# Dilated stage's maxima stored branch by branch, gate steps behind a block, two evictions ahead of a gate, blocks without a GpSimd drain

## The chip, the cores and the metric

The kernel runs on one core of one Trainium2 chip. The metric is the device time of one execution in microseconds, shown as the median of several runs.

## What is computed

One inference step of a one-layer hybrid decoder, for a prompt of 2048 tokens and 8 samples of 8 tokens, model width 1024, in float32. After an RMSNorm one projection `h @ w_in` gives the inputs of three mixers: an mLSTM matrix memory (4 heads of 64), a dilated window attention (6 heads of 64) and a stick-breaking attention (6 heads of 64). Their outputs go through `w_out`, an RMSNorm and the residual, then a squared-ReLU MLP of width 4096. The parts that the change touches, cut from the reference:

```python
# mLSTM: gates and chunk scan, chunks of 128 tokens
ig = ia + b_igate;  lf = log_sigmoid(fa + b_fgate)
b = cumsum(lf);     logw = where(causal, b[:, None] - b[None, :] + ig[None, :], -inf)
m_t = maximum(b + m, max(logw));  s = (q @ k.T) * exp(logw - m_t)
...
ya = rmsnorm(h_a) * g_mlstm * sigmoid(o_gate)

# dilated attention: three branches share q, k, v; joined by their softmax denominators
for window, dil in ((128, 1), (512, 4), (2048, 16)):
    s = (qs @ kk.T) * scale          # blocks of 128 queries x 256 keys, banded
    mx = max(s);  p = exp(s - mx);  den = sum(p)
    o = (p @ vv) / den;  lse = mx + log(den)
out = sum(softmax(lse over branches) * o)
```

## The kernel before

The program is a row of eight stages, each a `nc.Block` with its own semaphores. Within a block each engine has its own instruction list, written out by hand, and waits on semaphores. The stages in order: projection with the prompt's mLSTM (lines 111 to 990, names `p_`), stick-breaking of the prompt (`pc_`), dilated attention of the prompt (`pb_`), then three sample stages (`ms_`, `sd_`, `sc_`), the mixing with `w_out`, and the MLP. A block ends when every engine has drained and passed a barrier; then GpSimd clears the stage's semaphores (line 84) and a second barrier follows (line 85).

**Projection.** Three passes over 17 token tiles (16 of the prompt, one of the samples). A pass has the columns of one group of mixers, cut into three blocks `b` of 344 or 384 columns; a block is 24 matmuls, 8 slices of the width by three products of high and low parts, into one PSUM bank. ScalarE evicts each block (line 628) into `PT`, TensorE turns the q and k heads by three transposes a block (line 869), VectorE copies them out (line 787), and SyncE stores. In the first two passes blocks use four banks, in the third two, because the mLSTM chunks use the others.

The gate values of all chunks are prepared in the second pass, in steps that go to and fro between VectorE and TensorE. VectorE does a step at the end of its list of tiles 4, 6, 8, 10, 11, 12, 13 and 15, after the head copies of that tile; TensorE does the small matmuls `gates(0)` to `gates(4)` (lines 876 to 890) at the start of tiles 7, 9, 11, 12 and 13, each behind a wait on the count `pre_v` of VectorE. In the third pass tile `t` also carries chunk `t` of the mLSTM: ScalarE does `gate(t + 1)` (the output gate of the next chunk, three activations, which waits for that chunk's load) before the tile's evictions and `decay(t + 1)` (four activations, which waits for VectorE's `masked`) before the second. At tile 0 it does `gate(0)`, `decay(0)` and `gate(1)` first. Chunk 1's and chunk 2's loads go out when the second pass is done, since they land where its weights lie.

**Dilated attention.** Six heads. A head has three branches of 16 units, taken as 8 pairs each. For each head TensorE computes scores once for the maxima (`natural`, line 1705, branch by branch) and VectorE reduces them to `MX` (line 1647); this runs 36 pairs ahead of the second scores. The maxima of branch 0 and 1 must be put in the token order of branch 2, which is done through HBM: SyncE stores them into `scratch_bm` (one store for branch 0 with one number a packet, four for branch 1), waits for all five, and reads them back as `MR` (line 1480). VectorE joins them (`joint`, lines 1654 and 1658), SyncE stores the result and spreads it to `MB`, and the second scores subtract it. VectorE's list has `joint(0)` after pair 31, before the last four of the first 36. The queue of SyncE at the start of the stage:

```python
load_qk(1)
load_v(sp, 0, (2, 0))      # V of branch 2, V of branch 0; ScalarE issues branch 1's
for h in range(HB):
    if h >= 2:
        load_v(sp, h, (2, 0, 1))
    maxima(h)
    spread(h)
    ...
```

Of the kernel before, what the change touches and what calls it, by code (L numbers as in the profile page):

```python
# [14 lines left out]
P = 128  # L15
# [89 lines left out]
def project_phase(nc, A, S, O, F):  # L105
# [5 lines left out]
    with ExitStack() as ctx:  # L111
# [132 lines left out]
        qk_ok = m.sem("qk_ok")  # L244
        block = ctx.enter_context(nc.Block())

# [284 lines left out]
        def _(act):  # L531
# [57 lines left out]
            for v in range(3 * TILES):  # L589
# [12 lines left out]
                if p == 2 and t == 0:  # L602
                    act.wait_ge(mm_ok, 6 * TILES)
                    gate(0)
                    decay(0)
                if p == 2 and t + 1 < NCH:
                    gate(t + 1)
                for b, (a, e) in enumerate(PASSES[p]):
                    if b == 1 and p == 2:
                        if t >= 1:  # L610
                            norm(t - 1)
                        if t + 1 < NCH:
                            decay(t + 1)
                    if b == 2 and p == 0 and t + 1 < TILES:
                        high(t + 1)
                    if b == 0 and p == 0:
                        act.wait_ge(rs_ok, t + 1)
                    if b == 0 and v >= 2 and t < NT:
                        act.wait_ge(p_out[v % 2], stored(*divmod(v - 2, TILES)))
                    act.wait_ge(mm_ok, 3 * v + b + 1)  # L620
                    if t == NT:
                        if b == 2:
                            act.wait_ge(blk_ok, 3 * v + 1)
                        act.activation(lower(v, b, e - a), PP[bank(3 * v + b)][NS:P, 0:e - a], ACT.Copy, scale=rs[NS:P, t:t + 1]).then_inc(low_ok, 1)
                        continue
                    if b == 0 and t == 0 and p:
                        act.wait_ge(blk_ok, 3 * v)
                    act.activation(PT[v % 2][:, a - o:e - o], PP[bank(3 * v + b)][:, 0:e - a], ACT.Copy, scale=rs[:, t:t + 1]).then_inc(blk_ok, 1)  # L628
            state(act, 1)

# [217 lines left out]
        def _(pe):  # L848
# [100 lines left out]
            for v in range(3 * TILES):  # L949
                p, t = divmod(v, TILES)  # L950
                s = v % 3
                if p == 1 and t in (7, 9, 11, 12, 13):
                    gates((7, 9, 11, 12, 13).index(t))
                if p == 0:
# [4 lines left out]
                for b, (a, e) in enumerate(PASSES[p]):  # L959
# [4 lines left out]
                    for k in range(KD):  # L964
# [5 lines left out]
                        if t < NT:  # L970
                            ins = pe.matmul(out, HL[s][:, k, :], wh, start=False, stop=(k == KD - 1))  # L971
                    ins.then_inc(mm_ok, 1)
                    if b == 1 and p == 0 and t + 1 < TILES:
                        turn_tile(t + 1)
# [58 lines left out]
def stick_prompt_phase(nc, A, S, O, F, H):  # L1033
# [40 lines left out]
    with ExitStack() as ctx:  # L1074
# [38 lines left out]
        y_out = H.y_out  # L1113
        block = ctx.enter_context(nc.Block())

# [201 lines left out]
def dilated_prompt_phase(nc, A, S, O, T, H):  # L1317
# [61 lines left out]
    with ExitStack() as ctx:  # L1379
# [48 lines left out]
        y_out = T.y_out  # L1428
        block = ctx.enter_context(nc.Block())

# [29 lines left out]
        def _(sp):  # L1460
            def load_qk(h):
# [3 lines left out]
                for dst, src in ((Q[i], S["qkT"][GB + g]), (K[i], S["qkT"][GB + 3 + g])):  # L1465
                    for a in range(2):
                        sp.dma_start(dst[a * HD:(a + 1) * HD, :], src[d, 0:SEQ]).then_inc(qk_in[i], 16)

            def maxima(h):
                s = h % 2  # L1470
                sp.wait_ge(mx_ok, 2 * upto(h, 15))
                with nc.allow_non_contiguous_dma(reason="one maximum each"):
                    sp.dma_start(S["bm"][h, 0, :].rearrange("(n i) -> i n", i=P), MX[s][:, 0, :]).then_inc(m_out[s], 16)
                for n in range(4):
                    sp.dma_start(S["bm"][h, 1, n * 512:(n + 1) * 512].rearrange("(i f) -> i f", f=4),
                                 MX[s][:, 1, 4 * n:4 * n + 4]).then_inc(m_out[s], 16)
                sp.wait_ge(m_out[s], 16 * 5 * (h // 2 + 1))
                if h >= 2:
                    sp.wait_ge(mj_ok, h - 1)
                sp.dma_start(MR[s][:, :, :], S["bm"][h, 0:2, :].rearrange("b (p f) -> p b f", f=TILE)).then_inc(r_in[s], 16)  # L1480
# [21 lines left out]
            load_qk(1)  # L1502
            load_v(sp, 0, (2, 0))
            for h in range(HB):
                if h >= 2:
                    load_v(sp, h, (2, 0, 1))
                maxima(h)
                spread(h)
                if h == 0:
                    load_qk(2)  # L1510
                    load_v(sp, 1, (2, 0, 1))
                if h >= 2:
                    store(h - 2)
                if h >= 1 and h + 2 < HB:
                    load_qk(h + 2)
                if h == 4:
                    sp.wait_ge(T.padded, 1)
                    T.load(sp, A, S)
# [394 lines left out]
def mlstm_sample_phase(nc, A, S, O, W, T):  # L1913
# [6 lines left out]
    with ExitStack() as ctx:  # L1920
# [41 lines left out]
        y2_ok, y3_ok, yt_ps, yt_ok = (m.sem(x) for x in ("y2_ok", "y3_ok", "yt_ps", "yt_ok"))  # L1962
        block = ctx.enter_context(nc.Block())

# [265 lines left out]
def dilated_sample_phase(nc, A, S, O, W, G):  # L2230
# [12 lines left out]
    with ExitStack() as ctx:  # L2243
# [25 lines left out]
        passed = m.sem("passed")  # L2269
        block = ctx.enter_context(nc.Block())  # L2270

# [212 lines left out]
def stick_sample_phase(nc, A, S, O, W, G, E):  # L2484
# [9 lines left out]
    with ExitStack() as ctx:  # L2494
# [62 lines left out]
        y_out = E.s_out  # L2557
        block = ctx.enter_context(nc.Block())
        qs, ks = S["qkT"][GC:GC + 3, :, SEQ:SEQ + NS], S["qkT"][GC + 3:GC + 6, :, SEQ:SEQ + NS]
# [425 lines left out]
def mix_out_phase(nc, A, S, O, E):  # L2985


    with ExitStack() as ctx:
# [41 lines left out]
        x1_out, h_out = E.x1_out, E.h_out  # L3030
        block = ctx.enter_context(nc.Block())
        TILES = NT + 1
# [182 lines left out]
def mlp_phase(nc, A, S, O, E):  # L3215
# [72 lines left out]
    with ExitStack() as ctx:  # L3288
# [52 lines left out]
        y_out = m.sem("y_out")  # L3341
        block_ = ctx.enter_context(nc.Block())

# [590 lines left out]
```

## Time and profile before

| | us |
|---|---|
| median of 3 runs | 3605.03 |
| lowest, highest | 3599.06, 3608.02 |
| the profiled execution | 3601.67 |
| its span, first to last instruction | 3600.1 |

The profile is one execution. Its lines give engines as PE (TensorE), PEld (its weight loads), DVE (VectorE), ACT (ScalarE), POOL (GpSimd) and SP (SyncE); a `q` behind the name is the engine's sequencer, which also issues transfers. `L968` is line 968 of the kernel, `out<-in` are tiles, and a group in square brackets or behind a bar tells how long the engine stood idle before and what ended it. PEclk is the granted clock of TensorE, 1.00 at 2.4 GHz and 0.50 at 1.2 GHz.

### The profile page before, as it was taken

The numbers are of one execution on the slowest core, as the hardware profiler recorded it, in microseconds if no ns is written. First come the engines' busy times: TensorE is split into PE (matmuls) and PEld (weight loads), VectorE is DVE, ScalarE is ACT, GpSimd is POOL, SyncE is SP. The second block draws the span as 40 slices with busy tenths as digits, with TensorE's granted clock in tenths as the row PEclk, the third lists the DMA queues.
The fourth block names the chain that finished last, engine by engine and source line by source line (L and its number), as shares of the span: only waits on it lengthen the run. The fifth ranks groups of instructions, "written<-read, shape, count | busy, mean of one in ns | idle before, by whom it ended". The sixth has DMA issues, their size and how long they took to land. (4 is left out here: it accounts for less than half of the span.)

```text
span 3600.1 us, 61533 instructions
## 1 busy us (share of the span) xinstructions
PE 3375.1 (94%) x22189; PEld 2941.3 (82%) x22189; DVE 1951.7 (54%) x4014; ACT 1550.4 (43%) x3079; POOL 715.7 (20%) x994
## 2 busy tenths in 40 slices
PE   8999999989997999879989979999989999899997
PEld 7999999954444887456658769999989999899997
DVE  2211134469996442446665555666656565846564
ACT  3321122268884444235442235444454344545342
POOL 0111112146773345024430110000100000100000
PEclk9999999989997999999999989999999999999998
DMA  5664356521014542769975544343444343422222
GB/s 201 215 216 154 134 188 203 174 76 45 7 36 86 90 83 94 287 219 357 355 259 163 176 151 134 113 159 117 148 154 132 125 151 120 160 76 83 70 68 82
DMA packets 433980, 527.76 MB, mean 147 GB/s; under 512 B 93425, under 2 KB 370546, under 8 KB 429202
## 3 DMA queue, kind: packets, MB, share of 16 engines
q1 hardware_dynamic: 405236, 410.19, 37.1%
q10 hardware_dynamic: 12076, 63.43, 5.1%
q0 software_dynamic: 16384, 50.35, 3.8%
q8 instruction: 179, 2.93, 0.3%
q14 instruction: 105, 0.86, 0.1%
HBM read 430.08 MB, written 143.91 MB: 159 GB/s over the span
## 5 line engine op out<-in xcount | busy, mean ns | idle before, releaser
L3792 PE MATMUL p_DP<-p_UH,p_WH 128*128 128x352 f32 x1536 | 498.7, 325 | 20.4 <-issue 14.2
L3793 PE MATMUL p_DP<-p_UL,p_WH 128*128 128x352 f32 x1536 | 497.4, 324 | 0.0
L3794 PE MATMUL p_DP<-p_UH,p_WL 128*128 128x352 f32 x1536 | 497.2, 324 | 0.0
L3792 PE MATMUL p_UP<-fc_TH,p_WH 128*128 128x352 f32 x1344 | 438.5, 326 | 27.0 <-DVE p_WL L3690 15.1
L3793 PE MATMUL p_UP<-fc_TL,p_WH 128*128 128x352 f32 x1344 | 436.5, 325 | 0.0
L3794 PE MATMUL p_UP<-fc_TH,p_WL 128*128 128x352 f32 x1344 | 436.0, 324 | 0.0
L968 PE MATMUL p_PP<-p_WH,p_HH 128*128 128x384 f32 (+1 forms) x1224 | 419.4, 343 | 8.7 <-DVE p_HL L654 4.4
L969 PE MATMUL p_PP<-p_WL,p_HH 128*128 128x384 f32 (+1 forms) x1224 | 408.0, 333 | 0.0
L971 PE MATMUL p_PP<-p_WH,p_HL 128*128 128x384 f32 (+1 forms) x1152 | 384.0, 333 | 0.0
L3792 PEld LDWEIGHTS p_DP<-p_UH,p_WH 128*128 128x128 f32 x1536 | 291.5, 190 | 22.5 <-issue 20.6
L628 ACT ACTIVATE p_PT<-p_PP,p_rs 128x384 f32<-128x384 f32 (+1 forms) x144 | 82.2, 570 | 503.9 <-PE p_PP L971 503.9
L3731 DVE TENSOR_TENSOR p_acc<-p_DP,p_acc 128x352 f32<-128x352 f32 x336 | 171.0, 521 | 227.3 <-PE p_DP L3794 227.2
L3793 PEld LDWEIGHTS p_DP<-p_UL,p_WH 128*128 128x128 f32 x1536 | 291.7, 190 | 0.0
L3794 PEld LDWEIGHTS p_DP<-p_UH,p_WL 128*128 128x128 f32 x1536 | 291.3, 190 | 0.0
L3792 PEld LDWEIGHTS p_UP<-fc_TH,p_WH 128*128 128x128 f32 x1344 | 254.9, 190 | 31.4 <-DVE p_WL L3690 17.8
L1143 POOL TENSOR_TENSOR pc_W<-pc_G,pc_PR 128x512 f32<-128x512 f32 (+2 forms) x240 | 245.6, 1039 | 102.4 <-DVE pc_PR L1242 93.4
L3793 PEld LDWEIGHTS p_UP<-fc_TL,p_WH 128*128 128x128 f32 x1344 | 254.9, 190 | 0.0
L3794 PEld LDWEIGHTS p_UP<-fc_TH,p_WL 128*128 128x128 f32 x1344 | 254.8, 190 | 0.0
L968 PEld LDWEIGHTS p_PP<-p_WH,p_HH 128*128 128x128 f32 x1224 | 232.8, 190 | 12.7 <-DVE p_WL L644 5.8
L969 PEld LDWEIGHTS p_PP<-p_WL,p_HH 128*128 128x128 f32 x1224 | 233.1, 190 | 0.0
L787 DVE COPY p_QK<-p_QP 128x384 f32<-128x384 f32 (+1 forms) x85 | 49.6, 583 | 327.1 <-PE p_QP L869 327.1
L971 PEld LDWEIGHTS p_PP<-p_WH,p_HL 128*128 128x128 f32 x1152 | 218.9, 190 | 0.0
(469 smaller groups left out, 6664.9 us busy)
## 6 DMA issues: line engine op xcount, KB each, us to landing
fc_WU<-in_w_up SPq DMA_DIRECT2D x48, 1024.0 KB, 5.4
p_WD<-in_w_down SPq DMA_DIRECT2D x192, 256.0 KB, 2.9
cw_K<-in_cache_sb_k SPq DMA_DIRECT2D x192, 192.0 KB, 4.0
cw_V<-in_cache_sb_v POOLq DMA_DIRECT2D x192, 192.0 KB, 5.4
out_s_wk<-in_cache_win_k ACTq DMA_DIRECT2D x64, 382.5 KB, 3.5
out_s_wv<-in_cache_win_v ACTq DMA_DIRECT2D x64, 382.5 KB, 4.2
p_HH<-scratch_xh SPq DMA_DIRECT2D x34, 512.0 KB, 4.6
p_HL<-scratch_xl SPq DMA_DIRECT2D x34, 512.0 KB, 5.4
```

Of the source, the lines that this page charges most:

```text
L628: act.activation(PT[v % 2][:, a - o:e - o], PP[bank(3 * v + b)][:, 0:e - a], ACT.Copy, scale=rs[:, t:t + 1]).then_inc(blk_ok, 1)
L787: dve.tensor_copy(QK[v % 2][:, 3 * i:3 * i + k, :], QP[n % 2 if p < 2 else 0][:, 0:k, :]).then_inc(qk_ok, 1)
L968: pe.matmul(out, HH[s][:, k, :], wh, start=(k == 0), stop=False)
L969: ins = pe.matmul(out, HH[s][:, k, :], wl, start=False, stop=(t == NT and k == KD - 1))
L971: ins = pe.matmul(out, HL[s][:, k, :], wh, start=False, stop=(k == KD - 1))
L1143: pool.tensor_tensor(W[x % NW][:, i, h, 0:w], G[u % NR][:, 0:w], PR[x % 2][:, i, h, 1:w + 1], ALU.mult).then_inc(w_ok, 1)
L3731: dve.tensor_tensor(a, down_bank(i), a, ALU.add).then_inc(ev_v, 1)
L3792: pe.matmul(out, hi, rhi, start=first, stop=False, skip_group_check=True)
L3793: pe.matmul(out, hi, rlo, start=False, stop=False, skip_group_check=True)
L3794: return pe.matmul(out, lo, rhi, start=False, stop=last, skip_group_check=True)
```

## The change

- In the second pass of the projection TensorE does each gate step after the tile's first block, not before it.
- In the third pass, at tile 0, ScalarE does `gate(1)` and `decay(1)` after it has evicted blocks 0 and 1. For all other tiles nothing moves.
- In the dilated stage a new function `straight(h)` stores branch 0's maxima, after a wait for that branch's eight pairs; `maxima(h)` keeps the four stores of branch 1, the wait and the read. For head 0 `straight(0)` stands ahead of both V loads, and V of branch 0 is loaded between the stores of branch 1 and the wait for them. For the other heads `straight(h)` stands directly before `maxima(h)`.
- All eight blocks are opened with `no_gpsimd_drain=True`: the other engines still drain at the end, the barrier is made of semaphores alone, and GpSimd doesn't drain there. The drains at the clearing of the semaphores and at the barrier behind it are kept.

```diff
-        block = ctx.enter_context(nc.Block())
+        block = ctx.enter_context(nc.Block(no_gpsimd_drain=True))
...
-                if p == 2 and t + 1 < NCH:
+                if p == 2 and 0 < t and t + 1 < NCH:
                     gate(t + 1)
                 for b, (a, e) in enumerate(PASSES[p]):
                     if b == 1 and p == 2:
                         if t >= 1:
                             norm(t - 1)
-                        if t + 1 < NCH:
+                        if t and t + 1 < NCH:
                             decay(t + 1)
...
                     act.activation(PT[v % 2][:, a - o:e - o], PP[bank(3 * v + b)][:, 0:e - a], ACT.Copy, scale=rs[:, t:t + 1]).then_inc(blk_ok, 1)
+                    if p == 2 and t == 0 and b == 1:
+                        gate(1)
+                        decay(1)
...
                 p, t = divmod(v, TILES)
                 s = v % 3
-                if p == 1 and t in (7, 9, 11, 12, 13):
-                    gates((7, 9, 11, 12, 13).index(t))
...
                     ins.then_inc(mm_ok, 1)
+                    if p == 1 and b == 0 and t in (7, 9, 11, 12, 13):
+                        gates((7, 9, 11, 12, 13).index(t))
...
+            def straight(h):
+                sp.wait_ge(mx_ok, 2 * upto(h, 7))
+                with nc.allow_non_contiguous_dma(reason="one maximum each"):
+                    sp.dma_start(S["bm"][h, 0, :].rearrange("(n i) -> i n", i=P), MX[h % 2][:, 0, :]).then_inc(m_out[h % 2], 16)
+
             def maxima(h):
                 s = h % 2
                 sp.wait_ge(mx_ok, 2 * upto(h, 15))
-                with nc.allow_non_contiguous_dma(reason="one maximum each"):
-                    sp.dma_start(S["bm"][h, 0, :].rearrange("(n i) -> i n", i=P), MX[s][:, 0, :]).then_inc(m_out[s], 16)
-                for n in range(4):
-                    sp.dma_start(S["bm"][h, 1, n * 512:(n + 1) * 512].rearrange("(i f) -> i f", f=4),
-                                 MX[s][:, 1, 4 * n:4 * n + 4]).then_inc(m_out[s], 16)
+                with nc.allow_non_contiguous_dma(reason="four maxima each"):
+                    for n in range(4):
+                        sp.dma_start(S["bm"][h, 1, n * 512:(n + 1) * 512].rearrange("(i f) -> i f", f=4),
+                                     MX[s][:, 1, 4 * n:4 * n + 4]).then_inc(m_out[s], 16)
+                if h == 0:
+                    load_v(sp, 0, (0,))
                 sp.wait_ge(m_out[s], 16 * 5 * (h // 2 + 1))
...
             load_qk(1)
-            load_v(sp, 0, (2, 0))
+            straight(0)
+            load_v(sp, 0, (2,))
             for h in range(HB):
                 if h >= 2:
                     load_v(sp, h, (2, 0, 1))
+                if h:
+                    straight(h)
                 maxima(h)
```

## Rows read from the trace of the kernel before

**Rows 1.** The page, busy time and share of each engine.

```profile
PE 3375.1 (94%) x22189; PEld 2941.3 (82%) x22189; DVE 1951.7 (54%) x4014; ACT 1550.4 (43%) x3079; POOL 715.7 (20%) x994
```

**Rows 2.** Windows of 25 us: busy by engine (instructions), granted clock, DMA share, GB/s.

```profile
375.00:400.00 25.00, 21.94 (x121) 21.53 (x120) 3.84 (x11) 2.33 (x4) 3.21 (x1) 0.93 0.37 126
400.00:425.00 25.00, 20.64 (x113) 19.98 (x112) 4.53 (x12) 2.33 (x4) 0.00 (x0) 0.93 0.37 117
...
475.00:500.00 25.00, 19.96 (x118) 19.24 (x118) 7.67 (x20) 7.32 (x20) 5.44 (x9) 0.93 0.65 210
```

**Rows 3.** Waits of TensorE from 318 to 425 us: total, times, longest.

```profile
PE p_HP L887 <- DVE p_EX L704: 3.5, 1, 3.5
PE p_HP L883 <- DVE p_PM L696: 3.1, 1, 3.1
PE p_HP L880 <- DVE p_aa L690: 1.3, 1, 1.3
PE p_HP L890 <- DVE p_GT L707: 0.8, 1, 0.8
PE p_HP L876 <- DVE p_lf L685: 0.8, 1, 0.8
```

**Rows 4.** Timeline of TensorE: start, duration, line, and the idle time before.

```profile
337.07 0.49 PE L869 MATMUL p_QP<-p_ident,p_PT 128*128 128x128 f32 x3
...
341.58 0.49 PE L869 MATMUL p_QP<-p_ident,p_PT 128*128 128x128 f32 x3
...
484.20 0.90 PE L869 MATMUL p_QP<-p_ident,p_PT 128*128 128x128 f32 x3 [5.04 <-ACT p_PT L628]
```

**Rows 5.** A window of 4.2 us, matmuls into `PP` alone: busy, clock, DMA.

```profile
386.70:390.90 4.20, 4.20 (x17) 0.65 1.03 344
```

**Rows 6.** Timeline of ScalarE and VectorE, first tile of the third pass.

```profile
482.23 0.42 ACT L563 ACTIVATE p_OG<-p_AX 128x256 f32<-128x256 f32 x1 [8.54 <-DMA p_AK<-scratch_qkT]
...
483.56 0.58 ACT L628 ACTIVATE p_PT<-p_PP,p_rs 128x384 f32<-128x384 f32 x1
484.04 1.26 ACT L574 ACTIVATE p_DT<-p_DM,p_aa 128x128 f32<-128x128 f32 x4
...
479.83 0.69 DVE L724 TENSOR_TENSOR p_DM<-p_mask,p_GB 128x512 f32<-128x512 f32 x1 [7.47 <-DMA p_GB<-scratch_gT]
480.44 0.75 DVE L732 SCALAR_TENSOR_TENSOR p_ST<-p_HP,p_DT 128x256 f32<-128x256 f32 x2
```

**Rows 7.** SyncE's queue in the dilated stage, from 1100 to 1240 us.

```profile
1117.28 9.38 SPq L1454 DMA_DIRECT2D pb_VV<-out_p_wv  x1
1126.71 4.49 SPq L1473 DMA_DIRECT2D scratch_bm<-pb_MX  x1
...
1143.83 0.37 SPq L1480 DMA_DIRECT2D pb_MR<-scratch_bm  x1
...
1165.05 0.62 SPq L1473 DMA_DIRECT2D scratch_bm<-pb_MX  x1
...
1178.40 0.37 SPq L1480 DMA_DIRECT2D pb_MR<-scratch_bm  x1
```

**Rows 8.** VectorE there: the first maximum of branch 1, and the joined maxima.

```profile
1121.48 0.29 DVE L1647 CUSTOM_DVE_ANT_0 pb_junk<-pb_ST,pb_mask 128x128 f32<-128x128 f32 x1
...
1145.51 0.17 DVE L1654 TENSOR_TENSOR pb_MR<-pb_MR 128x16 f32<-128x16 f32 x1 [10.21 <-DMA pb_MR<-scratch_bm]
```

**Rows 9.** Instructions of L2243 (dilated sample stage's end) and L84: ns min/median/max, first and last start.

```profile
L2243 POOLq DRAIN  x1: 5659/5659/5659, 1576.7 to 1576.7; - x1
L2243 ACTq DRAIN  x1: 150/150/150, 1577.4 to 1577.4; - x1
...
L84 POOLq DRAIN  x13: 55/93/179, 749.7 to 3599.3; - x13
```

**Rows 10.** DMA from 1126 to 1144 us, GB/s in 40 slices.

```profile
GB/s 159 193 235 204 224 225 219 219 216 220 218 218 218 145 36 16 1 5 4 4 4 37 0 0 0 1 0 0 0 0 0 0 0 0 0 0 0 0 0 0
```

**Rows 11.** Window of the dilated stage: busy by engine, clock, DMA share, GB/s.

```profile
1175.00:1400.00 225.00, 224.41 (x1431) 185.59 (x1430) 83.01 (x406) 106.04 (x230) 98.27 (x219) 0.98 0.40 72
```

More of the change, by code:

```diff
@@ L1113, in stick_prompt_phase @@
         y_out = H.y_out
-        block = ctx.enter_context(nc.Block())
+        block = ctx.enter_context(nc.Block(no_gpsimd_drain=True))
         def turned(eng, v, h):
@@ L1428, in dilated_prompt_phase @@
         y_out = T.y_out
-        block = ctx.enter_context(nc.Block())
+        block = ctx.enter_context(nc.Block(no_gpsimd_drain=True))
         def found(a):
@@ L1962, in mlstm_sample_phase @@
         y2_ok, y3_ok, yt_ps, yt_ok = (m.sem(x) for x in ("y2_ok", "y3_ok", "yt_ps", "yt_ok"))
-        block = ctx.enter_context(nc.Block())
+        block = ctx.enter_context(nc.Block(no_gpsimd_drain=True))
         @block.gpsimd
@@ L2269, in dilated_sample_phase @@
         passed = m.sem("passed")
-        block = ctx.enter_context(nc.Block())
+        block = ctx.enter_context(nc.Block(no_gpsimd_drain=True))
         @block.gpsimd
@@ L2557, in stick_sample_phase @@
         y_out = E.s_out
-        block = ctx.enter_context(nc.Block())
+        block = ctx.enter_context(nc.Block(no_gpsimd_drain=True))
         qs, ks = S["qkT"][GC:GC + 3, :, SEQ:SEQ + NS], S["qkT"][GC + 3:GC + 6, :, SEQ:SEQ + NS]
@@ L3030, in mix_out_phase @@
         x1_out, h_out = E.x1_out, E.h_out
-        block = ctx.enter_context(nc.Block())
+        block = ctx.enter_context(nc.Block(no_gpsimd_drain=True))
         TILES = NT + 1
@@ L3341, in mlp_phase @@
         y_out = m.sem("y_out")
-        block_ = ctx.enter_context(nc.Block())
+        block_ = ctx.enter_context(nc.Block(no_gpsimd_drain=True))
         def up_bank(i):
```

## The prediction

> **What bounds the kernel now.** I read the page first: TensorE is busy 94% of the span [rows 1], so only time in which it stands still, or runs at the lower of its clock levels, can be won back. Then I cut the span into stretches of 25 us and looked for those where its busy time falls short. Inside the projection there are three, two in the second pass and one at the start of the third, each with a granted clock of 0.93 beside the missing time [rows 2]. The waits of TensorE between 318 and 425 us name the cause of the first two: five waits on VectorE, all at the small matmuls of the gate steps [rows 3]. The third is a wait of 5.04 us at the first head transposes of the third pass, put down to an eviction by ScalarE [rows 4], and ScalarE was not slow, it stood in a wait on a load [rows 6]. Next I read the start of the dilated stage in SyncE's queue and on VectorE: VectorE waits 10.21 us for the joined maxima, and TensorE, which needs VectorE's maxima to free its banks, stands with it [rows 7, 8]. Last come the ends of the eight blocks, by the line that closes each [rows 9].
>
> **1. Gate steps behind a tile's first block.** Before, steps 0 to 4 stand ahead of a tile's first block, and wait for a chain on VectorE that starts only when the last head transposes of the tile before are copied out: 0.8, 1.3, 3.1, 3.5 and 0.8 us, 9.5 us in all [rows 3]. After, the block runs first. A block with its following three transposes takes 341.58 - 337.07 = 4.5 us, some 4.2 without the transposes [rows 4]. The longest wait is 3.5, so each chain is done 0.7 us or more before TensorE comes to ask: all 9.5 us go. The steps' own matmuls only move. VectorE's later steps read what these give from its place after the tile's last head copies, two blocks further on, so nothing becomes late there; ScalarE's evictions and the loads keep their spacing of 13 us a tile.
>
> **2. The clock behind those waits.** The stretches with the 3.1 and 3.5 us waits have a granted clock of 0.93 [rows 2]: 25 x 0.07 / 0.5 = 3.5 us at the lower level, 1.2 of 2.4 GHz. Right after the first, 4.2 us hold 17 matmuls where a full-speed block holds 24 [rows 5]. The counts price it: at 6 matmuls in a busy microsecond, 21.94 us should hold 131 and hold 121 [rows 2], 10 x 0.17 = 1.7 us lost. The stretches with waits of 0.8 and 1.3 us show no fall that I had to add. Without the two long waits TensorE stays at the upper level: 3.4 us more. Ends of this cost: nothing if the clock falls anyway, 3.5 if not; I take 3.4, because nothing else but the waits is special to these stretches.
>
> **3. First tile of the third pass.** Before, ScalarE's gate for chunk 1 stands ahead of all evictions of tile 0. Its load lands at 482.23, so block 0, long finished, is evicted only at 483.56, and TensorE waits 5.04 us [rows 4, 6]. TensorE stopped at 484.20 - 5.04 = 479.2, the end of block 1; block 0 ended a block earlier, near 474.7. After, both are evicted as they finish, and then the gate waits. What is queued behind that wait on ScalarE: the gate (3 x 0.43), the decay (1.26) and the eviction of block 2 [rows 6]. Gate and decay end at 482.2 + 1.3 + 1.3 = 484.8. Block 2, started without the wait, ends near 479.2 + 0.8 for the small matmuls + 4.2 = 484.2, is evicted by 485.5, and its bank is wanted only when tile 1 gets to its second block, near 489. VectorE, which must multiply chunk 0's scores before the copy that frees the transposes, gets its own load at 479.83, ends the scores at 480.44 + 0.75 = 481.2 [rows 6], and has 3 us for the copy before the next transposes ask at 484. So the 5.0 us go. The granted clock is 0.93 here too [rows 2]; part of that low stretch lies in the wait itself, and I count 1.4 us. Next late would be chunk 2's load, issued right behind chunk 1's: to hold back the first eviction of tile 1, due at 489, it would have to land 5 us after chunk 1's. If that happened the wait would come back shorter, never longer, because no load is issued later than before. Parts 1 to 3: 9.5 + 3.4 + 5.0 + 1.4 = 19.3 us. TensorE has no other wait till the pass ends, so they reach the stage's end.
>
> **4. Maxima of branch 0 stored on their own.** Before, SyncE issues V of branch 2, V of branch 0 (9.38 us in its queue), then the five stores from 1126.71 on, waits for them, and reads back at 1143.83; VectorE goes on at 1145.51, 1.7 us later [rows 7, 8]. After, branch 0's store goes out at 1121.5, when VectorE starts branch 1 [rows 8], ahead of both V loads; V of branch 2 follows, then the four stores of branch 1 (their maxima are done near 1126.5), then V of branch 0, then the wait. No DMA is added or dropped. What the stores no longer stand behind is V of branch 0. The transfer rates show its size: over 18 us from 1126, in slices of 0.45, the engines move V at some 218 GB/s up to slice 14, near 1132.3, so its 128 x 1024 x 4 bytes = 524 KB are 2.4 us; the small packets end by slice 22, near 1136, and then almost nothing moves for 7 us, until the stores are home [rows 10]. Bounds: the four stores cannot be home before they are issued at 1127, and VectorE comes to the read at 1135.3, so at most the whole 10.2 us go. From below, heads 1 to 5 need 13.4 us from the first store's issue to the read's (1165.05 to 1178.40) [rows 7]; counted from the second group's issue at about 1128, that is 1141.4, a gain of 2.4. And nothing, if the read, now queued behind V of branch 0, gives it back. I take 4.5 us: the 2.4 of one V load, and 2.1 because the silence after branch 0's store now lies under V of branch 2; that is the side of the heads 1 to 5. SyncE's wait on the first eight pairs makes V of branch 2 about 5.7 us late; it is needed when the values begin, which the joined maxima hold back past 1145, and V is through by then. For heads 1 to 5 the store keeps its place in the queue: zero. From 1175 to 1400 TensorE is busy 224.4 of 225 us [rows 11], so what the start gains, the end gains.
>
> The Trainium skill (DMA: Bandwidth & Descriptors, Anatomy of one DMA) puts the fixed cost of a transfer near 2 us. By that estimate the four stores would be home before VectorE asks, all 10.2 us would go, and the sum would be 29.7 instead of 24; the 7 us of silence above speak against it, so I keep the row.
>
> **5. No GpSimd drain.** At seven of the eight ends another engine is last. At the end of the dilated sample stage GpSimd is: its drain runs from 1576.7 for 5.66 us, to 1582.4, while ScalarE's, the last of the others, ends at 1577.6 [rows 9]. So 1582.4 - 1577.6 = 4.8 us look free. But GpSimd is issuing loads until then, and the semaphores' clearing, two steps on, has a drain on GpSimd of its own (13 of them, 55 to 179 ns now, because each comes after one that has done the waiting) [rows 9]. I expect that one to take the wait over: it would end at the same 1582.4 and only the first barrier's passage, 0.2 us, is saved. Ends: 0 and 4.8; I take 0.2. The other seven: nothing.
>
> **Sum.** 19.3 + 4.5 + 0.2 = 24.0 us. The profiled execution took 3601.67 (span 3600.1 and 1.6 around it): 3577.7. It lies 3.4 below the median of the three runs, 3605.03, which would give 3581.0. I predict 3579, between the two.
>
> **Rivals.** (a) The drain is really gone: the clearing's drain doesn't wait, the next stage starts 4.6 us earlier than I say: 3574.4. For it: the drains at the clearing are short everywhere. Against: none of them was ever asked while loads were being issued. Chance 0.14. (b) The dilated stage gains nothing: the read of the maxima sits in one queue behind V of branch 0 and lands no earlier than before, 1145.5. For it: the total of packets ahead of the read is what it was. Against: the stores' 7 us of silence now overlap V's transfer. 3583.5, chance 0.14. The Trainium skill (DMA: Bandwidth & Descriptors, Queues, rings and completion order) says that a semaphore increment lands only after every earlier write of that DMA engine; by that rule the read's semaphore has V of branch 0 ahead of it, which is this rival, and the trace of before has no read in that place. (c) The gate steps' waits are not hidden, since VectorE's chain moves with TensorE, and parts 1 and 2 fail: 3579 + 12.9 = 3592, chance 0.03; the chain's start, the last copy of the tile before, speaks against it. (d) Slower: with fewer pauses TensorE loses its upper clock in the busy stretches. There is a trace of it: in the dilated stage it is busy 224.4 of 225 us at a granted 0.98 [rows 11], 9 us at the lower level, 4.5 us of work. Each such stretch of 3.5 us costs 1.7; to be slower than before by 10.8 us it needs (24 + 10.8) / 1.7 = 20 more of them. Chance 0.02.
>
> **How the numbers follow.** My forecast has 0.67, own range 3574 to 3585. The spread of the three runs, 9 us, is in that. The range for 8 in 10 reaches over (a) and (b) with that spread: 3568 to 3589. About 0.3%, 10.8 us, is what a measurement of this kernel tells from no change. Faster by more: 0.94 (all of forecast, a and b, half of c); within: 0.04; slower: 0.02.
>
> **What would show it.** Right: no wait of TensorE between 318 and 500 us above 0.5 us, and a clock of 1.00 there; the projection ends 19 us earlier; VectorE's wait for the joined maxima 5 to 6 us; GpSimd's drain gone at the dilated sample stage's closing line and one of about 4.7 us at the clearing. Wrong: a wait at the gate matmuls after block 0; a new wait of ScalarE on chunk 2's load; the read of the maxima issued early but landing late; low-clock stretches in new places of the projection.

## The result and the profile after

| | before | after |
|---|---|---|
| median of 5 runs, us | 3603.93 | 3577.82 |
| lowest, highest | 3599.06, 3608.02 | 3575.44, 3585.73 |
| profiled execution, its span | 3601.67, 3600.1 | 3575.62, 3574.0 |

The ratio is 0.9934, 95% interval 0.9917 to 0.9951. The forecast was 3579. The total came out within 1.2 us, but not its terms. The table cuts both profiled executions at the barrier that closes each stage (line 85); times in us.

| stage | before | after | difference | forecast |
|---|---|---|---|---|
| projection | 750.9 | 731.8 | -19.1 | -19.3 |
| stick-breaking | 361.8 | 361.8 | 0 | 0 |
| dilated | 308.2 | 308.2 | 0 | -4.5 |
| first sample stage | 28.3 | 28.3 | 0 | 0 |
| dilated sample stage | 133.9 | 129.1 | -4.8 | -0.2 |
| last sample stage | 302.7 | 304.3 | +1.6 | 0 |
| mixing (with two short clearings) | 234.8 | 231.7 | -3.1 | 0 |
| MLP | 1479.4 | 1478.8 | -0.6 | 0 |

So parts 1 to 3 were right, part 4 gave nothing, part 5 gave 4.8, and the two misses cancel by luck. Each column is one execution. In a second profile of the changed kernel, at the end of the experiments, the dilated stage takes 305.7 us and the dilated sample stage 132.5, so single differences of 2 to 3 us in this table can be the granted clock of one execution.

**The projection.** TensorE has no wait at all between 300 and 520 us. The windows of [rows 2], again with busy time by engine, granted clock, DMA share and GB/s:

```profile
375.00:400.00 25.00, 25.00 (x149) 24.48 (x148) 7.08 (x20) 3.49 (x6) 3.20 (x1) 1.00 0.45 143
400.00:425.00 25.00, 25.00 (x149) 24.54 (x148) 4.10 (x8) 3.33 (x6) 3.20 (x1) 1.00 0.44 151
...
475.00:500.00 25.00, 25.00 (x165) 24.20 (x164) 9.53 (x25) 7.17 (x20) 6.06 (x10) 1.00 0.64 203
```

Busy 25.00 of 25 at a clock of 1.00 in all three, where 21.94, 20.64 and 19.96 at 0.93 stood. ScalarE at the first tile of the third pass, in order of time, answers to [rows 6]:

```profile
461.60 0.58 ACT L628 ACTIVATE p_PT<-p_PP,p_rs 128x384 f32<-128x384 f32 x1 [0.56 <-issue]
466.55 0.58 ACT L628 ACTIVATE p_PT<-p_PP,p_rs 128x384 f32<-128x384 f32 x1 [4.38 <-PE p_PP L972]
469.70 0.42 ACT L563 ACTIVATE p_OG<-p_AX 128x256 f32<-128x256 f32 x1 [2.57 <-DMA p_AK<-scratch_qkT]
...
470.92 1.26 ACT L574 ACTIVATE p_DT<-p_DM,p_aa 128x128 f32<-128x128 f32 x4
472.10 0.56 ACT L628 ACTIVATE p_PT<-p_PP,p_rs 128x384 f32<-128x384 f32 x1
472.60 0.42 ACT L563 ACTIVATE p_OG<-p_AX 128x256 f32<-128x256 f32 x1
```

Blocks 0 and 1 are evicted when they are done, and the gate behind them still waits 2.57 us for chunk 1's load, now with nothing due. Gate and decay end at 472.2, block 2 is evicted at once, and the gate of chunk 2 at 472.60 waits for nothing: the next load is not late.

**The dilated stage's start.** SyncE's queue and VectorE's joined maxima answer to [rows 7, 8]:

```profile
1102.43 0.38 SPq L1475 DMA_DIRECT2D scratch_bm<-pb_MX  x1
1102.85 6.81 SPq L1455 DMA_DIRECT2D pb_VV<-out_p_wv  x1
1109.70 9.75 SPq L1482 DMA_DIRECT2D scratch_bm<-pb_MX  x4
1119.49 0.53 SPq L1457 DMA_DIRECT2D pb_VV<-out_p_wv  x1
1125.11 0.37 SPq L1489 DMA_DIRECT2D pb_MR<-scratch_bm  x1
```

```profile
1126.87 0.17 DVE L1666 TENSOR_TENSOR pb_MR<-pb_MR 128x16 f32<-128x16 f32 x1 [10.72 <-DMA pb_MR<-scratch_bm]
```

Branch 0's store goes out 8.8 us after the stage's start at 1093.6, as forecast (1121.5 of 1112.7 before). But V of branch 2 then sits 6.81 us in the queue and the four stores 9.75, where they took 3.42 before. VectorE's wait is 10.72 us against 10.21. Three of the runs below keep the old order of this stage and have waits of 10.2, 10.4 and 11.3 us; two more have the new order unchanged, with 8.9 and 9.1. The stage takes 306.7 to 308.2 us in the four profiles with the old order and 305.7 to 308.4 in the three with the new one. The transfer rates over the same phase as [rows 10], from 1106.85 in slices of 0.45 us, show what moves:

```profile
GB/s 135 171 226 131 23 8 1 0 0 0 0 1 0 4 30 109 39 31 32 34 32 11 27 35 31 39 40 56 115 222 198 108 103 131 137 105 101 156 155 148
```

The bulk loads end with slice 3, at 1108.7. Then come four silent microseconds, and from slice 16 to slice 26, 1114 to 1119, V of branch 2 trickles at 11 to 40 GB/s. In the kernel before V moved at some 218 GB/s [rows 10], with the small stores behind it and not ahead.

**The end of the dilated sample stage.** The instructions of its closing line and of the clearing answer to [rows 9]; the last row is TensorE's first work in the next stage:

```profile
L2255 ACTq DRAIN  x1: 161/161/161, 1558.3 to 1558.3; - x1
```

```profile
L84 POOLq DRAIN  x13: 55/83/174, 730.5 to 3573.2; - x13
```

```profile
1559.32 2.79 PE L2831 MATMUL sc_KTP<-cw_ident,cw_K 128*128 128x128 f32 x12 [3.13 <-PEq L85]
```

ScalarE's drain, 1558.3 + 0.16, is the last thing before the barrier. None of the thirteen drains at the clearing is longer than 0.17 us, so the wait has not moved there.

What the old drain waited for can be read from GpSimd's own queue, which carries the loads for the next stage. In the kernel before, the last packet of that queue ends 1580.66 us after the span's start and the drain at 1582.38, 1.72 us later. In the three other profiles that have this drain the distance is 1.72, 1.72 and 1.73 us. In the changed kernel the packets run on to 1561.2, two microseconds into the next stage. That queue's packets, MB and share from 1559.2 to 1562 us:

```profile
q0 software_dynamic: 113, 0.32, 28.4%
```

The equal distances suggest that the block's drain waits until these loads have landed (to the last packet of ScalarE's stores, the other transfers under way, they vary from 1.0 to 1.4 us). The clearing's drain, 0.08 us long with the same loads under way, doesn't wait for them. No run with other loads has tested this.

### The profile page after: what moved, and what is told of

The parts are those of the page before. It is cut to its first block and busy times, and to the rows that moved or that the text cites. A ratio compares the mean times of both kernels' runs of the same rounds, so it can differ in the third digit from the quotient of the medians.

```text
span 3574.0 us, 61557 instructions
## 1 busy us (share of the span) xinstructions
PE 3368.9 (94%) x22189; PEld 2935.4 (82%) x22189; DVE 1952.5 (55%) x4014; ACT 1549.6 (43%) x3079; POOL 716.2 (20%) x994
## 5 line engine op out<-in xcount | busy, mean ns | idle before, releaser
L3804 PEld LDWEIGHTS p_UP<-fc_TH,p_WH 128*128 128x128 f32 x1344 | 255.4, 190 | 30.8 <-DVE p_WL L3702 17.8
```

What stands on the lines that cost most here:

```text
L3804: pe.matmul(out, hi, rhi, start=first, stop=False, skip_group_check=True)
```

## The experiments

All are timed against the kernel before on the same chip. A stage's length is cut as in the table above. A low stretch is a time in which TensorE's granted clock is 0.50, that is 1.2 GHz.

**Gate steps alone.** The kernel before with the steps moved:

```diff
-                if p == 1 and t in (7, 9, 11, 12, 13):
-                    gates((7, 9, 11, 12, 13).index(t))
...
                     ins.then_inc(mm_ok, 1)
+                    if p == 1 and b == 0 and t in (7, 9, 11, 12, 13):
+                        gates((7, 9, 11, 12, 13).index(t))
```

> The kernel before with one thing changed: the gate steps of the second pass stand behind a tile's first block. Theory (parts 1 and 2 of the forecast): the five waits of 9.5 us and the two low-clock stretches behind the two long ones (3.4 us) all go, 12.9 us: span near 3587.2, the projection's closing line 12.9 us earlier, clock 1.00 from 318 to 425 us, and the wait of 5.0 us at the first tile of the third pass stays, with a low clock behind it. Rival 1: the clock has nothing to do with the waits, 9.5 us only. Rival 2 (c of the forecast): VectorE's chain moves with TensorE, the waits come back behind block 0, nothing gained.

Measured: 3592.3 against 3602.8, ratio 0.9966 (0.9956 to 0.9976). The projection closes 12.3 us earlier (738.6), for 12.9 forecast. All five waits are gone and one wait is left between 300 and 500 us; the window behind it has busy time, clock and DMA as above:

```profile
PE p_QP L869 <- ACT p_PT L628: 5.1, 1, 5.1
```

```profile
469.00:476.00 7.00, 5.35 (x21) 5.36 (x22) 1.69 (x5) 3.13 (x9) 2.33 (x4) 0.53 0.23 80
```

This settles rivals 1 and 2: the two low stretches of the second pass went with their waits. The wait at the third pass, unchanged in length, is now accompanied by some 6.8 us at 1.2 GHz where the profile before had 3.4: one wait costs one or two such stretches, so each of these prices is uncertain by 1.7 us.

**First tile of the third pass alone.** The kernel before with the conditions `0 < t` and `t` on `gate(t + 1)` and `decay(t + 1)`, and

```diff
+                    if p == 2 and t == 0 and b == 1:
+                        gate(1)
+                        decay(1)
```

> The kernel before with part 3 alone: ScalarE's second gate and decay behind its first two evictions of the third pass. Forecast: the wait of 5.0 us at the first head transposes of the pass goes, and 1.4 us of low clock with it: the projection closes 6.4 us earlier, at 744.5 instead of 750.9, while the five waits of the second pass (9.5 us) and their two low stretches stay. Rival: the low clock there stays, 5.0 us only, 745.9. In the run with the gate steps alone the low clock behind this wait was 6.8 us long instead of 3.4, so the kernel with both parts gained 6.8 to 7.4 us over it.

Measured: 3596.2 against 3605.0, ratio 0.9979 (0.9969 to 0.9988). The projection closes at 745.6, 5.3 us earlier: the 5.0 are there. The low stretch here is gone as well, but its gain does not show, because the wait of 3.1 us in the second pass now has two of them:

```profile
375.00:400.00 25.00, 21.94 (x115) 21.47 (x114) 3.84 (x11) 2.70 (x5) 3.20 (x1) 0.86 0.39 134
...
465.00:490.00 25.00, 25.00 (x159) 24.49 (x158) 10.02 (x25) 9.58 (x23) 5.18 (x11) 1.00 0.75 229
```

A clock of 0.86 in 25 us is 7 us at the lower level, where 0.93 was 3.5. Singly the parts gave 12.3 and 5.3, together 19.1: with no wait left there is nothing for a low stretch to stand behind.

**GpSimd's drain put back at one stage.** The changed kernel with `nc.Block()` at the dilated sample stage alone.

> The changed kernel with GpSimd's drain put back at the end of the dilated sample stage alone. Theory 1: the drain had held that end by itself, and the clearing's drain waits for nothing: GpSimd drains until some 4.8 us behind ScalarE's drain again, the stage closes at 1563.4 instead of 1558.6 after the span's start. In the next stage, which took 303.8 us before and 305.35 in the changed kernel, 1.6 us come back if the low clock at its start ends at its own time and not with the work: net 3.2 to 4.8 us slower than the changed kernel. Theory 2: the drain is as short as the clearing's, and the 4.8 us came from somewhere else: the stage closes at 1558.6 and nothing changes.

Measured: 3584.6 against 3602.8, ratio 0.9944 (0.9926 to 0.9962). The stage takes 136.0 us, 6.9 more than in the changed kernel's first profile. The instructions of its closing line, and the stage as one window here and then in the changed kernel:

```profile
L2255 POOLq DRAIN  x1: 5365/5365/5365, 1559.9 to 1559.9; - x1
L2255 ACTq DRAIN  x1: 151/151/151, 1561.9 to 1561.9; - x1
```

```profile
1429.97:1565.99 136.02, 112.55 (x1160) 71.15 (x1160) 51.84 (x111) 36.55 (x65) 17.39 (x32) 0.91 0.73 261
```

```profile
1430.06:1559.15 129.09, 108.65 (x1160) 68.29 (x1160) 51.84 (x111) 36.55 (x65) 17.39 (x32) 0.96 0.77 270
```

The drain ends at 1559.9 + 5.4 = 1565.3, ScalarE's at 1562.1: it holds the end 3.2 us. The other 3.7 are TensorE's: the same 1160 matmuls take 112.55 us instead of 108.65, at a clock of 0.91 instead of 0.96. The changed kernel's second profile, without this drain, has 112.19 us of them at 0.93 and a stage of 132.5 us, 3.5 less than here. Theory 1 holds in kind, theory 2 is out; the price of the drain depends on how late ScalarE is.

**No drain alone.** The kernel before with `no_gpsimd_drain=True` on all eight blocks and nothing else.

> The kernel before with part 5 alone: no GpSimd drain at any of the eight ends. Theory from the run with the drain put back: the dilated sample stage takes 129.1 us instead of 133.9 (131 to 132.6 if one or two more stretches of low clock fall into it), its end is set by ScalarE's drain, and no other stage closes earlier. In the whole, 3 to 5 us faster, which the clock's stretches may hide. Rival (the forecast's own step): the clearing's drain takes the wait over, 133.7.

Measured: 3600.8 against 3605.0, ratio 0.9989 (0.9980 to 0.9999). The stage takes 129.1 us, as forecast by this theory, and closes behind ScalarE's drain (1576.9) with nothing of GpSimd's there but the barrier's two semaphore steps:

```profile
L2243 POOLq EVENT_SEMAPHORE  x2: 17/17/17, 1577.2 to 1577.2; - x2
```

Over all profiles this stage takes 133.7 to 136.0 us in the four with the drain and 129.1 to 132.6 in the ten without it.

The next stage gives a third of it back. The first 34 us of the last sample stage, in the kernel before and in this one:

```profile
1583.07:1617.07 34.00, 29.02 (x223) 19.99 (x224) 21.74 (x59) 15.58 (x28) 5.89 (x14) 0.91 0.51 158
```

```profile
1577.80:1611.80 34.00, 28.83 (x216) 20.36 (x217) 21.10 (x57) 14.87 (x26) 5.32 (x13) 0.84 0.53 159
```

The stage starts 5 us earlier but the clock rises no earlier, so more of its start runs at 1.2 GHz: in the same 34 us 0.84 instead of 0.91, and 216 matmuls instead of 223. The whole stage took 302.7 and 302.8 us in the two profiles whose stage ahead took 133.7 to 133.9, and 304.2 to 304.3 in four of the five whose stage ahead took 129.1 to 129.3. Of 4.8 us won 1.5 are given back there. The fifth of them, with all of V on ScalarE's queue, took 307.5 with more low clock at its start. In the other seven profiles other low stretches fall in, and it takes 301.6 to 306.0.

**V of branch 0 behind the read.** The changed kernel, for head 0:

```diff
-                if h == 0:
-                    load_v(sp, 0, (0,))
                 sp.wait_ge(m_out[s], 16 * 5 * (h // 2 + 1))
...
                 sp.dma_start(MR[s][:, :, :], ...).then_inc(r_in[s], 16)
+                if h == 0:
+                    load_v(sp, 0, (0,))
```

> The changed kernel with head 0's V of branch 0 issued behind the read of the maxima. Theory 1 (rival b of the forecast): V of branch 0 in the queue holds the stores or the read back: the read is issued 2 to 4 us before 1125.1 and VectorE's 10.7 us wait shrinks by as much. Theory 2: the four stores are held by V of branch 2 and by the first store ahead of them (9.75 us of issue, from 1109.7 to 1119.5); V of branch 0 is issued behind them and costs the read at most 1 us: VectorE's wait stays at 9.7 to 10.7.

**Both V loads behind the read.** The same with `load_v(sp, 0, (2, 0))` there and none ahead.

> The changed kernel with head 0's V of branch 2 and of branch 0 both issued behind the read of the maxima. If V of branch 2 is what holds the four stores, they are issued from 1107.4 on at 0.43 us each and are home together with branch 0's store, whose increments landed at 1117.1 to 1119.3: the read is issued at 1118 to 1120 and VectorE goes on at 1121, 5 to 6 us earlier. If the small stores themselves are slow, whatever stands between them, the read stays near 1125. What comes behind: the store and the reads of the joined maxima now queue behind 1 MB of V (4096 packets, 8.4 us in the kernel before), so the joined maxima reach TensorE at about 1133 instead of 1130, and the stage ends no earlier, or up to 3 us later, in spite of the earlier read.

**Both behind the joined maxima.** `load_v(sp, 0, (2, 0))` after `spread(0)`, just ahead of `load_qk(2)`.

> The changed kernel with head 0's V of branches 2 and 0 issued behind the reads of the joined maxima, just ahead of head 2's loads. With both behind the read of the maxima, that read went out 6.4 us earlier, but the joined maxima, now behind 1 MB of V, made TensorE wait 3.7 us, and the dilated stage took 305.7 us against 308.15. Theory: that wait is V in the queue; with V behind the joined maxima too it goes, the joined maxima land near 1124.5, TensorE's wait for VectorE stays at about 5.4 us, and the stage takes 302 to 303.5 us. Rival: V, issued at 1123.5 and through by 1129 to 1130, is now late for the first values, which TensorE reaches about 6 us behind the joined maxima, near 1130: a wait on V of up to 2 us, stage 304 to 305.

The waits of VectorE for the read, in the changed kernel, in a second profile of it, and in these three in order (the run with GpSimd's drain put back, which has the changed kernel's order here, waits 8.9):

```profile
DVE pb_MR L1666 <- DMA pb_MR<-scratch_bm: 10.7, 1, 10.7
```

```profile
DVE pb_MR L1666 <- DMA pb_MR<-scratch_bm: 9.1, 1, 9.1
```

```profile
DVE pb_MR L1666 <- DMA pb_MR<-scratch_bm: 7.7, 1, 7.7
```

```profile
DVE pb_MR L1665 <- DMA pb_MR<-scratch_bm: 5.0, 1, 5.0
```

```profile
DVE pb_MR L1664 <- DMA pb_MR<-scratch_bm: 5.8, 1, 5.8
```

V of branch 0 costs the read 1.2 to 3.0 us, although the stores are issued ahead of it; V of branch 2 another 2 to 2.7. My theory 2 for the first of the three was wrong, and rival (b) of the forecast was right that V holds the maxima back. With no V ahead of them 5 to 6 us of wait remain. The single runs with V behind the read came to 3578.8 and 3578.6, the third kernel to 3579.5 (ratio 0.9929, 0.9912 to 0.9946): no gain over the changed kernel. In the second of the three the read is early and TensorE waits for what is late next, the joined maxima behind 1 MB of V:

```profile
1128.42 0.47 PE L1735 MATMUL pb_ST<-pb_MB,pb_neg 64*128 64x128 f32 x2 [3.74 <-DMA pb_MB<-scratch_bm]
```

With V behind these too, that wait is gone and one of 1.0 us for V takes its place, as its rival said. The stage's length can't settle it: 307.2, 305.7 and 305.4 us, but the changed kernel itself has 308.2 and, in the second profile, 305.7, and the run with the drain put back 308.4.

**All of V on ScalarE's queue.** `load_v(act, 0, (1, 2, 0))` on ScalarE, none of head 0 on SyncE.

> The changed kernel with all of head 0's V issued by ScalarE behind its V of branch 1, none on SyncE's queue. Theory 1: what held the stores is the order within SyncE's queue: the read goes out near 1119 as with V behind it, nothing is late, the stage takes 302 to 304 us. Theory 2: the 16 DMA engines are shared, and V's 4096 packets of 256 bytes from another queue slow the stores' packets and the keys of head 1 as much: the read near 1122 to 1125, ScalarE's roundings of head 1 up to 4 us later than 1108 because it is held in issuing, the stage takes 306 to 309 us.

Measured: 3577.4, ratio 0.9918 (0.9901 to 0.9934), the stage 307.8 us. ScalarE's issue of V of branch 1, then its first rounding of head 1:

```profile
1100.47 15.75 ACTq L1460 DMA_DIRECT2D pb_VV<-out_p_wv  x4
1116.27 0.63 ACT L1600 ACTIVATE pb_QH<-pb_Q 128x512 fp32r<-128x512 f32 x1 [18.65 <-issue]
```

Theory 2, and worse: ScalarE is held in issuing for 15.75 us, and head 1's rounding starts 24.3 us after the stage's start instead of 14.4. TensorE waits 9.1 us for it, while VectorE's wait for the read is down to 0.7 because it comes there late. The stores, alone in SyncE's queue, still let the read go only 30.3 us after the start, as in the changed kernel (31.5 and 29.6 in its two profiles), and not 25.7 or 26.6 as with V behind the read or behind the joined maxima. The Trainium skill (DMA: Bandwidth & Descriptors, Issuing engines are not separate DMA queues) says that spreading transfers over issuing engines saves only issue time; this run agrees, and here it lost that too.

**Branch 0's maxima in runs of 64 bytes.** The kernel with V behind the joined maxima, and

```diff
-                    sp.dma_start(S["bm"][h, 0, :].rearrange("(n i) -> i n", i=P), MX[h % 2][:, 0, :])...
+                    sp.dma_start(S["bm"][h, 0, :].rearrange("(i n) -> i n", i=P), MX[h % 2][:, 0, :])...
```

> The kernel with V behind the joined maxima, and branch 0's maxima stored in runs of 64 bytes (128 packets) instead of one maximum at a time (2048 packets of 4 bytes); they lie in another order in memory, so the joined maxima are wrong, and only the times are read. Theory 1: the 4-byte writes are what is slow: their packets end at 1110 and their increments land 3 to 9 us later. With 64-byte runs all five stores are home by 1112 to 1113, the read goes out 5 to 6 us earlier than with V behind the joined maxima alone, and VectorE waits less than 1 us in head 0; the stage takes 297 to 299 us. Theory 2: the silence belongs to the 16-byte stores or to any store: the read moves by less than 2 us.

Measured: 3565.1, one run; the stage takes 297.9 us. The joined maxima of this kernel stand in the wrong order, so only its times are read. SyncE's queue:

```profile
1102.10 0.33 SPq L1475 DMA_DIRECT2D scratch_bm<-pb_MX  x1
1107.08 2.27 SPq L1482 DMA_DIRECT2D scratch_bm<-pb_MX  x4
1110.98 0.37 SPq L1487 DMA_DIRECT2D pb_MR<-scratch_bm  x1
```

The read goes out 17.7 us after the stage's start instead of 26.6, VectorE doesn't wait at all, and the stage is 7.6 us shorter than its parent's. Theory 1: the silence is the 2048 writes of 4 bytes. The four stores of 16-byte packets are home 1.6 us behind the last one's issue.

**Turned in the read.** To keep the order right, the store stays in 64-byte runs and the read gathers single maxima:

```diff
-                sp.dma_start(MR[s][:, :, :], S["bm"][h, 0:2, :].rearrange("b (p f) -> p b f", f=TILE)).then_inc(r_in[s], 16)
+                sp.dma_start(MR[s][:, 1, :], S["bm"][h, 1, :].rearrange("(p f) -> p f", f=TILE)).then_inc(r_in[s], 16)
+                sp.dma_start(MR[s][:, 0, :], S["bm"][h, 0, :].rearrange("(q f n) -> n q f", n=TILE, f=TILE)).then_inc(r_in[s], 16)
...
-                dve.wait_ge(r_in[s], 16 * (h // 2 + 1))
+                dve.wait_ge(r_in[s], 32 * (h // 2 + 1))
```

> The kernel with V behind the joined maxima, branch 0's maxima stored in 64-byte runs, and turned into the right order where they are read: 2048 packets of 4 bytes read from memory in place of 2048 written. The result is the reference's again. Theory: only small writes are slow. The stores are home near 1111 as with the 64-byte runs, the two reads go out at once and land 2 to 4 us later, near 1114, VectorE waits 0 to 3 us in head 0, the dilated stage takes 298 to 300 us against 308.15, and the kernel is 8 to 10 us faster than the changed one, about 3569. Rival: 4-byte reads are as slow as 4-byte writes: the reads land 8 us after their issue, near 1119, and the stage takes 304 to 306 us as with V behind the joined maxima alone.

Measured: 3572.4, ratio 0.9911 (0.9896 to 0.9926). The stage takes 299.1 us. The median time from issue to landing of the transfers in it:

```profile
scratch_bm<-pb_MX SPq DMA_DIRECT2D x4, 2.0 KB, 2.0
pb_MR<-scratch_bm SPq DMA_DIRECT2D x2, 8.0 KB, 2.7
```

The plain read of both branches took 1.7 us to land (median of the kernel before). Here the plain read of branch 1 takes 2.0 us and the gathered one 3.45, which gives the median of 2.7; so 2048 packets of 4 bytes that are read cost some 1.7 us more. Written, they held the read back by 26.6 - 17.7 = 8.9 us. VectorE doesn't wait; TensorE waits 0.4 us for V.

**Turned in the read, V in the changed kernel's place.** The change of the read alone, on the changed kernel.

> The changed kernel in its own order (branch 0's store, V of branch 2, the other stores, V of branch 0, the read), with branch 0's maxima stored in 64-byte runs and turned in the read. Theory: V of branch 2 crawled at some 30 GB/s in the changed kernel because the 4-byte writes ahead of it were still on their way; without them its 524 KB pass at over 150 GB/s in 3 us, SyncE's issue of V and of the four stores takes under 7 us together instead of 16.6, the stores are home near 1113, and the read, behind V of branch 0, lands near 1116 to 1117: the stage takes 299 to 301 us, with no wait for V. Rival: V itself is slow whatever is ahead of it, and the read lands near 1122 to 1125: stage 305 to 308 us.

Measured: 3571.8, ratio 0.9906 (0.9891 to 0.9921), the stage 300.2 us. VectorE waits 3.0 us for the read. SyncE's queue, and the rates from 1102 to 1120 us in slices of 0.45:

```profile
1102.01 0.60 SPq L1455 DMA_DIRECT2D pb_VV<-out_p_wv  x1
1106.62 4.02 SPq L1482 DMA_DIRECT2D scratch_bm<-pb_MX  x4
1110.68 0.43 SPq L1457 DMA_DIRECT2D pb_VV<-out_p_wv  x1
1113.34 0.61 SPq L1489 DMA_DIRECT2D pb_MR<-scratch_bm  x1
```

```profile
GB/s 203 212 171 228 299 152 192 172 116 141 136 223 211 245 226 221 217 153 34 22 5 0 0 23 21 104 261 291 290 164 70 10 3 2 1 0 0 0 0 37
```

V of branch 2 takes 0.60 us to issue instead of 6.81 and runs at over 200 GB/s (slices 13 to 16; before them ScalarE's V of branch 1 shares the rate); V of branch 0 follows at up to 290. Theory confirmed: V was never slow, it stood behind the 4-byte writes.

**The changed kernel again**, on the same chip as the last two:

> The changed kernel as it is, once more on the chip of the two others. Its dilated stage, 308.15 us, and the other stages up to the mixing come back within 1 us where no other stretch of low clock falls into them; what moves between executions is that, in steps of 1.7 us for each 3.4 us at the lower level, and with it the total, within 3574 to 3586.

Measured: 3578.1, ratio 0.9927 (0.9914 to 0.9941). Its dilated stage took 305.7 us, 2.4 less than in the first profile, so the expectation of 1 us was too narrow: VectorE's wait was 9.1 instead of 10.7, and a low stretch near 1247 was missing. Its dilated sample stage took 132.5 us, 3.4 more than in the first profile and 1.4 less than before the change, with TensorE's clock at 0.93 instead of 0.96; what part 5 gives depends that much on the execution. Against it the two kernels that turn in the read are 5.7 and 6.3 us faster by their medians, and 6.7 and 5.6 in the stage; the intervals of the ratios overlap, so it is the stage that shows the gain.

## Why the prediction was right, and where it wasn't

**1, 2, 3: right.** The waits are gone, block 0 covers every one, and the parts together gave 19.1 us for 19.3. Taken singly, part 3 gave 5.3 for 6.4, and parts 1 and 2 12.3 for 12.9. The mis-sized term is the price of the clock, which came to one or two stretches per wait.

**4: wrong by 4.5 us.** VectorE waits 8.9 to 10.7 us in the three profiles with the changed order, 10.2 to 11.3 in the four with the old one, and the stage is no shorter. The step that failed is "the silence after branch 0's store now lies under V of branch 2". It does, and that is the harm: the queue behind the 4-byte writes comes to a crawl, V's issue is held 6.8 us, the four stores' 9.8, and they reach memory hardly earlier. From the issue of branch 0's store to the read 17.1 us pass in the kernel before, 16.9 and 17.8 in the two runs with no V behind that store, and 20.8 to 22.7 with the changed order. The store went out 5.1 us earlier, and most or all of that was lost to the V loads behind it. The sentence that put V at 218 GB/s took its rate from a place where no such write stood ahead. The second failed step is that V of branch 0 no longer matters behind the stores; it costs 1.2 to 3.0 us. Rival (b) gave the right result, zero, with V of branch 0 as its only cause. The read itself was not held: it landed 1.7 us after its issue, as before, and V of branch 0 had landed 0.6 us ahead of it. The estimate from the Trainium skill's fixed cost of 2 us (DMA: Bandwidth & Descriptors, Anatomy of one DMA) was right for the 16-byte stores as soon as no 4-byte write stood ahead, 2.0 us, and far off for those. The page gives its figure for transfers that GpSimd issues; these are SyncE's.

**5: wrong by 4.6 us in the first profile.** The step that failed is "I expect that one to take the wait over". The clearing's drain, with GpSimd's last load issued half a microsecond earlier, took 0.08 us, and the whole 4.8 us went, which was rival (a) and the upper bound. At the other ends nothing came, as forecast.

**What the sum left out.** 1.5 us came back as low clock at the start of the last sample stage, shown by the run with no drain alone. The mixing took 3.1 us less and the MLP 0.6; the mixing alone takes 233.7 to 236.6 us in the three profiles with GpSimd's drain at its end and 230.3 to 235.0 in the eleven without. That drain is not the last at this end, and I found no way by which it would act. A good part is the clock: the same 952 matmuls keep TensorE busy 211.7 us before and 209.9 after, and in the changed kernel's second profile 211.4, with a mixing of 231.9. Whether the change has a part in the rest is open. The misses are -0.2, -4.5 and +4.6, and 2.1 of the rest: 26.0 by the stages, 26.1 by the spans, for 24.0. That the total came within 1.2 us of the forecast is luck, since the two misses of some 4.5 us have opposite signs.

**Still open:** the rest of the mixing's 3 us, and a test of what GpSimd's drain at a block's end waits for. At this stage it started each time while the last load was being issued, took 5.4 to 6.0 us and ended 1.72 or 1.73 us behind the last packet of GpSimd's loads; another order of those loads was not tried.

## What to carry to other kernels

Before a transfer is put ahead of another, look at its packets and not at its bytes: 8 KB written as 2048 single numbers held what waited for it back by 9 us, and the same turn done in the read cost 1.7. A wait of TensorE can cost more than its length, by 1.7 us for each low stretch behind it, and a start that comes earlier can lose part of its gain to a clock that rises no earlier. And where one engine's drain is the last at a barrier, ask what it waits for, and look for the last packet of its own loads; a second drain behind it isn't bound to wait for the same.

## What was not expected of the hardware

- Small writes to memory and small reads from it differ: 2048 packets of 4 bytes kept the read 8.9 us back when written (issued 26.6 us after the stage's start, against 17.7), and cost some 1.7 us when read (3.45 us to land, against 1.7).
- While those writes were on their way, packets of 256 bytes in the same queue moved at 11 to 40 GB/s, and the issue of the next transfers was held in SyncE (6.81 us for one V load, 9.75 for four stores).
- The same wait of 5.0 to 5.1 us was followed by 3.4 us at 1.2 GHz in one execution and some 6.8 in another.
- The drain in the clearing took 0.08 us at the point where the block's own GpSimd drain took 5.4 to 6.0.
- The block's own drain ended 1.72 or 1.73 us behind the last packet of GpSimd's loads in all four profiles that have it, and with the drain left out those packets ran on into the next stage (to 1561.2, with the barrier at 1559.2).
